# Token-order stacks with strided operand reads in the dilated attention, and y transposes at the head of a step in the two full attentions

## The reference

```python
DIL_PATTERNS = ((128, 1), (512, 4), (2048, 16))

def dilated_group(q, k, v, dilation, half_steps, bias):
    b, s, h, d = q.shape
    L = s // dilation
    def to_sub(t):   # tokens of one class (position mod dilation) stand together
        return t.reshape(b, L, dilation, h, d).transpose(0, 2, 1, 3, 4).reshape(b * dilation, L, h, d)
    out, lse = banded_attention(to_sub(q)[:, :, :, None, :], to_sub(k), to_sub(v),
                                half_steps, half_steps, bias, None)
    ...

for gi, (w, r) in enumerate(DIL_PATTERNS):
    o, lse = dilated_group(cq5[:, :, gi], ck5[:, :, gi], cv5[:, :, gi], r, w // (2 * r), dil_bias[gi])
...
alpha = jax.nn.softmax(jnp.stack(lses, axis=0), axis=0)
y_c = jnp.sum(alpha[..., None] * jnp.stack(outs, axis=0).astype(jnp.float32), axis=0)
```

```python
logits = jnp.einsum("bqkgd,bskd->bkgqs", q_blk, k).astype(jnp.float32) * scale
p = jax.nn.softmax(logits, axis=-1).astype(v.dtype)
return jnp.einsum("bkgqs,bskd->bqkgd", p, v)
```

## Time and profile before

| | |
|---|---|
| time, median of 3 runs | 2976.74 us (2974.19 to 2979.92) |
| the profiled execution | 2975.42 us, its span 2973.6 us |
| PE busy | 2750.3 us, 92% |
| DVE busy | 1353.9 us, 46% |
| ACT busy | 1070.9 us, 36% |
| POOL busy | 626.2 us, 21% |
| dilated stage, passes 0 to 5, layer 0 | 709.1 to 1037.7 us |
| dilated stage, passes 0 to 5, layer 1 | 2180.9 to 2509.3 us |

### The profile page before, as it was taken

One profiled execution on the slowest core, in us unless ns is written; L12 is line 12 of the kernel. 1 busy time (PEld: TensorE's weight loads), 2 busy tenths in 40 slices (PEclk: granted clock), 3 DMA queues, 4 the chain that ended last, 5 costly groups with the idle time before them and its releaser, 6 DMA issues.

```text
span 2973.6 us, 36963 instructions
## 1 busy us (share of the span) xinstructions
PE 2750.3 (92%) x13836; PEld 2261.9 (76%) x13836; DVE 1353.9 (46%) x2871; ACT 1070.9 (36%) x2141; POOL 626.2 (21%) x337
## 2 busy tenths in 40 slices
PE   7899999899998889999979999999999889899997
PEld 6677787788777778877776778787887777788775
DVE  3574458523434355523145734584233443555222
ACT  4463117403444525511135621273134445254112
POOL 2101420132111122232220024201321112222321
PEclk9999999999999999999989999999999999999998
DMA  7000210021111131112050011100211112211122
GB/s 240 22 1 19 54 41 10 10 63 39 38 42 37 43 96 36 36 38 99 23 179 15 1 27 51 44 1 19 61 41 42 37 31 73 72 36 36 43 92 78
DMA packets 204198, 146.03 MB, mean 49 GB/s; under 512 B 21688, under 2 KB 187192, under 8 KB 203976
## 3 DMA queue, kind: packets, MB, share of 16 engines
q1 hardware_dynamic: 190188, 137.08, 16.1%
q10 hardware_dynamic: 13824, 6.49, 0.8%
HBM read 124.44 MB, written 27.49 MB: 51 GB/s over the span
## 4 chain that ended last, share of the span: by engine, by line
PE 79%; DVE 8%; ACT 5%; issue 4%; DMA 1%; POOL 1%; SPq 1%; ACTq 0%; POOLq 0%; DVEq 0%; another core or an unknown queue 0%
PE ps L892 19%; PE ps L855 9%; PE ps L857 9%; PE ps L856 9%; PE ps L997 5%; PE ps L1070 4%; PE ps L1038 4%; PE ps L954 4%; PE ps L955 4%; PE ps L956 4%; PE ps L1022 3%; PE ps L1007 2%; PE ps L999 2%; SPq L733 1%; DVE nm L1655 1%
## 5 line engine op out<-in xcount | busy, mean ns | idle before, releaser
L2059 POOL CAST wh<-wraw 128x1024 fp32r<-128x1024 f32 (+2 forms) x162 | 177.4, 1095 | 2242.3 <-PE ps L857 889.7
L855 PE MATMUL ps<-xh,wh 128*128 128x512 f32 x1120 | 441.7, 394 | 3.0 <-ACT pt_split L1547 2.2
L857 PE MATMUL ps<-xh,wl 128*128 128x512 f32 x1120 | 437.8, 391 | 0.0
L856 PE MATMUL ps<-xl,wh 128*128 128x512 f32 x1120 | 437.8, 391 | 0.0
L2061 POOL TENSOR_TENSOR wl<-wraw,wh 128x1024 fp32r<-128x1024 f32 (+2 forms) x162 | 421.6, 2602 | 13.0
L892 PE MATMUL ps<-xh,wh 128*128 128x512 f32 x864 | 362.6, 420 | 33.9 <-DVE bk_stack L1733 16.7
L892 PE MATMUL ps<-xh,wl 128*128 128x512 f32 x864 | 353.0, 409 | 0.0
L892 PE MATMUL ps<-xl,wh 128*128 128x512 f32 x864 | 352.1, 408 | 0.0
L855 PEld LDWEIGHTS ps<-xh,wh 128*128 128x128 f32 x1120 | 211.8, 189 | 47.0 <-ACT pt_split L1547 3.0
L857 PEld LDWEIGHTS ps<-xh,wl 128*128 128x128 f32 x1120 | 211.4, 189 | 45.0
L856 PEld LDWEIGHTS ps<-xl,wh 128*128 128x128 f32 x1120 | 211.9, 189 | 43.0
(11 more groups left out here) (213 smaller groups left out, 4758.5 us busy)
## 6 DMA issues: line engine op xcount, KB each, us to landing
wraw<-in_w_in_dram SPq DMA_DIRECT2D x128, 512.0 KB, 3.9
xres<-acc SPq DMA_DIRECT2D x2, 4096.0 KB, 15.8
toep<-toep_row SPq DMA_DIRECT2D x32, 256.0 KB, 10.8
wraw<-in_w_branch_dram SPq DMA_DIRECT2D x64, 128.0 KB, 3.8
wraw<-in_w_out_dram SPq DMA_DIRECT2D x16, 512.0 KB, 3.7
acc<-xres SPq DMA_DIRECT2D x16, 512.0 KB, 7.5
dil_out<-cst ACTq DMA_DIRECT2D x96, 66.0 KB, 1.6
att<-dil_out SPq DMA_DIRECT2D x48, 132.0 KB, 2.5
```

The lines of the kernel that those rows point to most:

```text
L855: pe.matmul(dst, ah, bh, start=i == 0, stop=False)
L856: pe.matmul(dst, ah, bl, start=False, stop=False)
L857: last = pe.matmul(dst, al, bh, start=False, stop=i == len(ks) - 1)
L2059: inc(pool.tensor_copy(high, raw), w_hi)
```

## The change

It has two parts. In C the copies and rests of all strides go to the stack in token order, and `logits` reads q and k with step r instead: `strided` turns a column number of class order into such a read. With r = 8 a class has 128 tokens, so the 256 columns of k are two classes, read one after the other; with r = 4 they are the one class of the unit, where the 256 columns before could reach into a neighbour's. In A and B the y transposes go to the head of the step on PE, and `gated` to the head of the step on DVE.

```diff
+        def strided(a, r, at, n):
+            c, l = divmod(at, S // r)
+            return a[:, c + r * l:c + r * (l + n - 1) + 1:r]
...
-                                at = min(k0, S - 2 * P)
-                                unit(cq_stack[hp][:, e, i * P:(i + 1) * P], ck_stack[hp][e][:, 0, at:at + 2 * P],
+                                if L == P:
+                                    at = min(k0, S - 2 * P)
+                                    c = at // L
+                                    spread = [ck_stack[hp][e][:, x, :].rearrange("p (l c) -> p c l", c=r)[:, c:c + 2, :]
+                                              for x in range(2)]
+                                else:
+                                    at = k0 // L * L + min(k0 % L, L - 2 * P)
+                                    spread = [strided(ck_stack[hp][e][:, x, :], r, at, 2 * P) for x in range(2)]
+                                unit(strided(cq_stack[hp][:, e, :], r, i * P, P), spread[0],
                                      table_g[:, hp * 2 + e, b0:b0 + nk], chunks, "act",
                                      st=i, head=hp * 2 + e, e=e, g=g, hp=hp, seen=(k0 - at, nk),
-                                     k_rest=ck_stack[hp][e][:, 1, at:at + 2 * P])
+                                     k_rest=spread[1])
...
         def fill_tokens(p, half):
 
-            if "g" not in p:
-                return lambda a: a[:, half * HALF:(half + 1) * HALF], lambda bank: bank
-            r = STRIDES[p["g"]]
-            w = HALF // r
-            return (lambda a: a.rearrange("p (c l) -> p l c", c=r)[:, half * w:(half + 1) * w, :],
-                    lambda bank: bank.rearrange("p (l c) -> p l c", c=r))
+            return lambda a: a[:, half * HALF:(half + 1) * HALF], lambda bank: bank
...
                     for s, begun, paired, tiles_of in dense_steps(b):
+                        for st in tiles_of(s - 6):
+                            pe.wait_ge(o_freed_dve, units[s - 6]["o_count"])
+                            y_transposes(next(y), yn[:, st % 2, :])
                         if begun(s):
                             if s - 2 >= u0:
                                 pe.wait_ge(exp_done, s - 1)
...
-                        for st in tiles_of(s - 6):
-                            pe.wait_ge(o_freed_dve, units[s - 6]["o_count"])
-                            y_transposes(next(y), yn[:, st % 2, :])
                         if begun(s - 2):
                             transposes_part(s - 2, 1)
...
                     for s, begun, paired, tiles_of in dense_steps(b) if n < 2 else []:
+                        for st in tiles_of(s - 6):
+                            gated(next(y), st)
                         if begun(s):
                             maxima(s, u0)
                         if paired(s - 5):
                             outputs(s - 6)
                             outputs(s - 5)
-                        for st in tiles_of(s - 6):
-                            gated(next(y), st)
```

More of the change, by code:

```diff
@@ L16 @@
 from contextlib import ExitStack
+import math
 import numpy as np
@@ L415, in unit @@
             ring, size = (2, S) if bias is None else (4, HALF if "sink" in more else 2 * P)
-            at, nk = more.get("seen", (0, k.shape[1]))
+            cols = math.prod(k.shape[1:])
+            at, nk = more.get("seen", (0, cols))
             bank = ps[:, s % 2 * w:(s % 2 + 1) * w, :].rearrange("p b n -> p (b n)")
             u = dict(q=q, k=k, bias=bias, chunks=chunks, who=who, groups=[], ring=ring, nk=nk,
-                     product_at=bank[:, 0:k.shape[1]], logits=bank[:, at:at + nk],
+                     cols=cols, product_at=bank[:, 0:cols], logits=bank[:, at:at + nk],
                      prob=prob_flat[:, s % ring * size:(s % ring + 1) * size], **more)
@@ L992, in logits @@
                     u = units[s]
-                    for c in range(0, u["k"].shape[1], HALF):
-                        w = min(HALF, u["k"].shape[1] - c)
+                    for c in range(0, u["cols"], HALF):
+                        w = min(HALF, u["cols"] - c)
                         rest = u.get("k_rest")
                         dst = u["product_at"][:, c:c + w]
-                        ins = pe.matmul(dst, u["q"], u["k"][:, c:c + w], start=True, stop=rest is None)
+                        whole = u["cols"] <= HALF
+                        ins = pe.matmul(dst, u["q"], u["k"] if whole else u["k"][:, c:c + w], start=True, stop=rest is None)
                         if rest is not None:
-                            ins = pe.matmul(dst, u["q"], rest[:, c:c + w], start=False, stop=True)
+                            ins = pe.matmul(dst, u["q"], rest if whole else rest[:, c:c + w], start=False, stop=True)
                     inc(ins, lg_ready)
```

## The result

The changed kernel takes 2931.23 us (median of 4 runs, 2927.97 to 2935.98), beside 2978.06 us for the kernel before in the same comparison. The ratio is 0.9841, with a 95% interval from 0.9821 to 0.9861: faster by 47 us, which is two thirds of the forecast's 68 us.

The account below looks back on a forecast made before the run. PE was taken as the bound, 79% of the span's chain, with standstills behind scattered k writes. Terms -96.4 + 30 - 1.7 = -68 us gave 2909 us, range 2870 to 2950 us.

Parts of the forecast that it names:

- The standstills: PE idle after k products in dilated passes 1 to 4, 3.52 and 1.89 us in pass 2, blamed on scattered writes.
- Rival 4: Standstills belong to emptying k itself and stay despite token-order stacks: 3005 us, chance 0.01.
- What the standstills are worth: Token-order stacks shorten passes 1 to 4 of both dilated stages, 96.4 us off, some third through the clock.
- the bullet list of what a pass would take: Dilated passes 1 to 4 without scattered writes, based on pass 0: 50.1, 50.5, 50.5 and 42.2 us.
- the 10.2 us that were taken off for pass 4: Pass 4's stride-8 units step in 2.82 us instead of 3.46, so 16 x 0.64 us less.
- The price of the strided read: Logits products on PE in passes 2 to 5: +0.14 us at stride 4, +0.10 at stride 8, 30 us in all.
- Part 2: y transposes at step head: B gains 0.40 us per tile, A loses 0.52 us per pair, together -1.7 us.
- rival 2: PE's moving strided read pays the addition of ACT's scattered copy, 60 us instead of 30: 2939 us, chance 0.18.
- Rival 1: Moving strided reads on PE free, 2879 us, or only stride 4 free, 2891 us; chance together 0.22.
- Rival 3: Strided stream on PE bound by 2.1 ns per element, 108 us more: slower, 2987 us, chance 0.11.

Follow-up runs that it names:

- the step in the bank: Kernel before, class-order stacks, but copies and rests write SBUF in runs and read PSUM with step 4 or 8; y transposes at head in B only: 2907.2 us.
- The kernel without gaps: Changed kernel with q and k read at contiguous columns, wrong tokens for strides 4 and 8, same work: 2911.09 us, ratio 0.9775.

## Why the prediction was right, and where it was off

- **The standstills come from the scattered writes of the k stacks: right.** With copies of 0.59 us they fall from 3.5 and 1.9 us to at most 1.08 us, and the clock in passes 1 to 4 is at 1.00. The kernel that gets rid of the scattering in another way, by the step in the bank, shows the same: at most 1.32 us. Rival 4 is out.
- **What the standstills are worth: 68.3 us instead of 96.4. This is the step that failed.** It was the bullet list of what a pass would take: 50.1, 50.5, 50.5 and 42.2 us. The kernel without gaps has 51.7, 54.3, 54.3 and 47.3 us, together 14.3 us more in a layer. The base was wrong: pass 0 is not a pass like the others. The stage's first units have no values and transposes of earlier units between them, so that pass 1, with the same units, takes 1.5 us more in the changed kernel and in the one without gaps (1.6 by the rounded windows). This error is in all four passes, some 6 us of the 14.3. Another 4.5 us are in passes 2 and 3, and 3.6 in pass 4. There I took 3.46 us as the step of both stride 1 and stride 4, from two neighbours of stride 4. The steps of stride 1, of which pass 0 is made, take 3.17 us where no value transposes stand between. So the passes of stride 4 are dearer than pass 0, and the 10.2 us that were taken off for pass 4 were counted from the wrong step, and for all 16 units, while the first ones still carry the work of stride 4 behind them. The sum for pass 4 also has a slip in it: it gives 2.6 us of standstill and adds 2.3.
- **The price of the strided read: right in kind, a little high.** Forecast +0.14 us at stride 4 and +0.10 at stride 8, measured +0.10 at both; in all 23.3 us instead of 30. That this came so close is in part luck. The load of the transposes grew by 0.07 and 0.05 us, the load of q at the same two steps by 0.12 us at either, and the moving operand by the same amount for 2, 4 and 8. So a strided load does not tell the price of a moving read, and no run shows a reason for its 0.10 us.
- **Part 2: right in both directions.** B gained 0.44 us for each tile (forecast 0.40), A lost 0.37 us for each pair (forecast 0.52). Only the standstills themselves came out shorter in the profile, 0.21 and 1.10 us, since the idle time is counted from the modelled end of a product. In all about 3 us by these steps, against 1.7. The span outside the two stages can't confirm it: it fell by 2.5 us, but five kernels with the same instructions ahead of the first dilated stage reach it after 707.2 to 712.6 us.
- **The sum.** -68.3 + 23.3 = -45.0 us in the two stages, and -2.5 us elsewhere, for -47.5 us of span, where the forecast had -96.4 + 30 - 1.7. The error of 28 us in the first term was made smaller by one of 7 us the other way in the second. That the measured 2931 us lie between the forecast (2909) and rival 2 (2939) is no support for rival 2: its price of the reads, 60 us, was not found.
- Rival 1, free reads, was wrong in either form: stride 4 pays, and so does a step of 2. Rival 3, 0.42 us for each product, was four times too dear.

Still open: why a step in the moving operand costs the same at 2, 4 and 8 elements, and whether the second product in the kernel with q alone strided is late because of its own load or because of that of the instruction behind it. That it lasts 0.13 us longer (0.41 us instead of 0.28), about what its load gained, speaks for its own. And PE waits somewhat longer between C and D for the combined outputs (8.92 us instead of 8.32 in layer 0, 7.84 instead of 5.70 in layer 1); no run was made on that.

## What to carry to other kernels

When an operand has to be regrouped on its way through ACT or DVE, let the instruction run along the order of its destination in SBUF and take the step on the side of PSUM; here that was free, while the scattered stack made ACT's instructions four fifths longer and DVE's, which also read it, half longer, and the strided read on PE doubled a product. When a stage is used as the base for its siblings, take one from the middle of the pipeline, and check the length of a step in each kind before subtracting. A wait for a buffer can be moved ahead of its cover: before transposes go to the head of a step, look up which engine frees their bank, and whether it does so in the middle or at the end of the step before.

## What the runs showed of the hardware

- A moving fp32r operand with a step of 2, 4 or 8 elements takes 0.20 to 0.22 us for 256 columns, without gaps 0.11 us. The size of the step makes no difference beyond that (changed kernel and the one with a step of 2).
- The load of a stationary fp32r operand of 128 columns takes 0.19 us without gaps, 0.20 us with a step of 2 and 0.31 us with a step of 4 or 8. The longer load costs up to 0.13 us beside a product of 0.11 us, and next to nothing beside one of 0.21 us (stages of 306.0 us with q strided and 305.4 without).
- Writes of ACT to SBUF: 0.59 us for 64x512 in a run, 0.62 us in pairs of neighbours, 1.07 us element by element. DVE's rests, which read and write the stack in the same pattern: 0.68 us in a run and in pairs, 1.05 us element by element.
- Reads of ACT and DVE from PSUM with a step of 4 or 8 elements take as long as without: 0.59 and 0.69 us.
